# Gate passes inside two attentions: eight at every second step instead of four at each step

## The chip, the cores and the metric

One core of one Trainium2 chip runs the whole program. The metric is the device time of one execution in microseconds (us); lower is better. The core's engines are named as in the profile: PE (matmuls), PEld (its weight loads), DVE (VectorE), ACT (ScalarE), POOL (GpSimd) and SP (which issues most transfers).

## What is computed

Two layers of a decoder trunk over 512 tokens of width 1024. In each layer four mixers (A a gated delta rule, B a latent attention, C a second delta rule, D a sparse attention over selected keys) read the normed input `h`; each mixer's output is projected to 1024 columns and weighted by its own sigmoid gate, which is a projection of `h` too. Cut to what matters here:

```python
p_gdn, p_mla, p_rwkv, p_dsa, p_gate = _split(h @ w_in[l], SLAB_SPLITS)
y_b = mla_mixer(p_mla, ...) @ w_out_mla[l]      # causal attention, 4 heads, 512 keys
y_d = dsa_mixer(p_dsa, ...) @ w_out_dsa[l]      # attention over 128 selected keys per query
g_a, g_b, g_c, g_d = _split(jax.nn.sigmoid(p_gate), GATE_SPLITS)
merged = g_a * y_a + g_b * y_b + g_c * y_c + g_d * y_d
x = x + merged @ w_o[l]
```

## The kernel before

Everything lies transposed in SBUF: 128 features on the partitions, 512 tokens along the row. The weights are cut into units of 1024 x 128, which the kernel takes in one fixed order (`unit_list`). For each unit SP loads a ring slot, ACT rounds it into a high part `w_hi` (L1197), POOL subtracts to get the low part `w_lo` (L462, two instructions), and PE makes 24 passes of 512 columns: 8 slices times high weights on `h_hi`, high weights on `h_lo`, low weights on `h_hi`. There are two slots for `w_hi` and `w_lo`, so ACT may round unit n+2 when PE is through with unit n.

All engines follow orders written out by hand and meet at semaphores. There are two attentions in each layer, "m" (mixer B) and "d" (mixer D), four in the program. Each has 16 tasks, one for each block of 128 queries and head: tasks 0 to 3 are 128 keys wide, 4 to 7 are 256, 8 to 11 are 384, 12 to 15 are 512. The loop has steps i = 0 to 18. The letters below stand for its parts.

- **S(i), S(i+1)**: at even i below 16 PE computes the scores of tasks i and i+1 (L790, L791). In "m" these contract over 96 rows and run one after the other; in "d" over 64 rows and side by side.
- DVE, at its own step i: **ss(i)** adds the mask and takes the row maximum (L1733), and then **n(i-1)** divides the task before by its row sum (a reciprocal, L1741, and a product from SBUF to SBUF, L1742). So n(j) of an odd task j stands behind ss(j+1) on DVE, and ss(j+1) waits for the scores that PE computes at step j+1.
- ACT, at its step i: **exp(i)** with its row sum (L1238); then the copy of the transposed task i-2 (L1245).
- **T(j)**: at step i = j+2 PE transposes task j into a bank of PSUM (L801, one matmul per 128 keys); it waits for n(j).
- **G**: gate passes, at each of the steps 1 to 18 a piece of four. `gate_pieces` (L596) makes three gate units in 18 pieces; L605 and L606 are high-weight passes, L611 are low-weight ones. They write the one bank `bank_f`. After the sixth piece of a unit ACT copies the bank (L1179) and rounds the next weight unit (L1197); the next unit's first pass waits for that copy.
- **Y(i-4)**: at even i from 4 on PE multiplies tasks i-4 and i-3 with the values (L812, tile 128x64) behind the gate piece; ACT copies the result (L1251).

The order on PE in a pair of steps, i even, is therefore: S(i), S(i+1); T(i-2); G; Y(i-4); T(i-1); G; and again. In "m" DVE also works on the selection of keys for mixer D at steps 5, 7, 9, 11 and 13 (`SPARE`; its lines are L2006 to L2021). At step 1 DVE merges one tile ("m") or two ("d") of the branch before.

Of the kernel before, what the change touches and what calls it, by code (L numbers as in the profile page):

```python
# [80 lines left out]
NU = len(UNITS)  # L81


GATE_STEPS = tuple(range(1, 19))


SPARE = {5: 1, 7: 2, 9: 1, 11: 2, 13: 2}
# [82 lines left out]
def build(nc, x_in, pos_in, wstream, par_in, const_in, tabs, x_dram, out):  # L170
    ctx = ExitStack()
    with ctx:
# [34 lines left out]
        def ar(q, shape, at=0):  # L207

            n = int(np.prod(shape))
            v = arena[:, q * T + at:q * T + at + n]  # L210
            if len(shape) == 1:
                return v
            names = " ".join("abcd"[:len(shape)])
            return v.rearrange(f"p ({names}) -> p {names}", **{k: s for k, s in zip("abcd", shape)})
# [81 lines left out]
        class Banks:  # L296
# [8 lines left out]
            def next(self, pool, done, value=None):  # L305


                i = self.used[pool] % len(self.pools[pool])
                self.used[pool] += 1
                sem_, emptied = self.reader[pool][i]  # L310
                if value is None:
                    self.counts[key[done]] = self.counts.get(key[done], 0) + 1
                    value = self.counts[key[done]]
                self.reader[pool][i] = (S[done], value)
                return self.pools[pool][i], sem_, emptied
# [23 lines left out]
        def quarter(i):  # L339

            return slice(i * C, (i + 1) * C)

        def merges_to(g):
# [29 lines left out]
        Dv = dict(  # L373
            rl=ar(11, (4, T)), scores=ar(2, (3, T)), wk=ar(5, (T,)), gt=ar(6, (T,)), eq=ar(30, (T,)), cum=ar(31, (T,)), bias=ar(7, (TT, T)),
            iq=ar(15, (4, T)), q=ar(19, (2, T)), k=ar(21, (2, T)), vf=ar(23, (2, T)), v=ar(25, (TT, 256)), tab=ar(27, (2, T)), ik=ar(29, (T,)),
            tmp=ar(35, (T,)), ss=ar(11, (4, T)), pt=ar(15, (4, TT, P)),
        )
        Mv = dict(
            cq=ar(37, (2, T)), sq=ar(39, (3, T)), rs=ar(23, (2, T)), q=ar(39, (4, T)), k=ar(11, (4, T)), v=ar(43, (TT, 256)),
            tab=ar(27, (2, T)), tmp=ar(29, (T,)), bias=ar(32, (T,)), kr=ar(33, (T,)), qr=ar(34, (T,)),  # L380
            ss=ar(15, (4, T)), pt=ar(33, (4, TT, P)),
        )
# [95 lines left out]
        def _(pe):  # L478
# [88 lines left out]
            def merge_outputs(slot, numbers):  # L567
                for n in numbers:
                    b, reader, emptied = banks.next("v", "mg_done")
                    pe.wait_ge(reader, emptied)  # L570
                    pe.wait_ge(out_here[n % OUT_RING], 16 * (n // OUT_RING + 1))
                    for k in range(2):
                        ins = mm(b[:], out_ring[:, n % OUT_RING, k, :], yo[:, slot, k, :], start=k == 0, stop=k == 1)  # L573
                    ins.then_inc(v_full, 1)

            def unit_pieces(l, wants, done):

                for want in wants:
                    g = begin_unit(want, l)
                    b, reader, emptied = banks.next("f", done)  # L580
                    pe.wait_ge(reader, emptied)
                    hi, lo = w_hi[:, g % SPLIT], w_lo[:, g % SPLIT]
                    for k in range(KT):
                        mm(b[:], hi[:, k, :], h_hi[:, k, :], start=k == 0, stop=False)  # L584
                        mm(b[:], hi[:, k, :], h_lo[:, k, :], start=False, stop=False)
                        if k in (0, 2, 3, 5, 6):
                            yield
                    pe.wait_ge(S["split_lo"], g + 1)
                    for k in range(KT):
                        ins = mm(b[:], lo[:, k, :], h_hi[:, k, :], start=False, stop=k == KT - 1)  # L590
                        if k in (1, 3):
                            yield
                    ins.then_inc(f_full, 1)
                    yield

            def gate_pieces(l, br, i, numbers):  # L596

                for j in range(3):
                    g = begin_unit(("merge", br, i + j), l)
                    numbers.append(merges_to(g))  # L600
                    b, reader, emptied = banks.next("f", "mg_raw")
                    banks.counts["mg_sig"] += 1
                    pe.wait_ge(reader, emptied)
                    for k in range(KT):
                        mm(b[:], w_hi[:, g % SPLIT, k, :], h_hi[:, k, :], start=k == 0, stop=False)  # L605
                        mm(b[:], w_hi[:, g % SPLIT, k, :], h_lo[:, k, :], start=False, stop=False)  # L606
                        if k % 2 == 1:
                            yield
                    pe.wait_ge(S["split_lo"], g + 1)
                    for k in range(KT):  # L610
                        ins = mm(b[:], w_lo[:, g % SPLIT, k, :], h_hi[:, k, :], start=False, stop=k == KT - 1)  # L611
                        if k == 3:
                            yield
                    ins.then_inc(f_full, 1)
                    yield
# [209 lines left out]
            for l in range(L):  # L825
# [86 lines left out]
                pieces = unit_pieces(l, [("gd", 6), ("gd", 7)], "g_z")  # L912
# [37 lines left out]
                pieces = unit_pieces(l, [("ds", 0), ("ds", 1)], "d_in")  # L950
# [75 lines left out]
                for half in range(2):  # L1026
                    b, reader, emptied = banks.next("a", "m_v")
                    pe.wait_ge(reader, emptied)
                    for t2 in range(2):
# [17 lines left out]
                numbers = []  # L1047
                pieces = gate_pieces(l, 1, 0, numbers)
                attention(l, "m", lambda h, qt: Mv["q"][0:96, h, qt * P:(qt + 1) * P],
                          lambda h, n: Mv["k"][0:96, h, 0:n], lambda i: next(pieces) if i in GATE_STEPS else None,  # L1050
                          lambda: merge_outputs(1, last[1:]))
                numbers.append(gate(l, 1, 3))
                pe.wait_ge(S["m_y"], at(l, "m_y", 8))
# [5 lines left out]
                numbers = []  # L1059
                pieces = gate_pieces(l, 3, 0, numbers)  # L1060
                attention(l, "d", lambda h, qt: Dv["q"][quarter(h % 2), h // 2, qt * P:(qt + 1) * P],
                          lambda h, n: Dv["k"][quarter(h % 2), h // 2, 0:n], lambda i: next(pieces) if i in GATE_STEPS else None,
                          lambda: merge_outputs(0, last))
                numbers.append(gate(l, 3, 3))
                pe.wait_ge(S["d_y"], at(l, "d_y", 8))
# [32 lines left out]
        def _(act):  # L1098
# [56 lines left out]
            sigs = [0]  # L1155
# [11 lines left out]

            def gate_done(i):

                return i in GATE_STEPS and GATE_STEPS.index(i) % 6 == 5  # L1170

            def piecewise_sig(l, i):

                if gate_done(i):
                    act.wait_ge(f_full, filled_f.next())
                    n = sigs[0] + GATE_STEPS.index(i) // 6
                    if n >= GATES:
                        act.wait_ge(S["mg_done"], n - GATES + 1)
                    act_fn(sg[:, n % GATES, :], filled_f.bank()[:], ACT.Copy).then_inc(S["mg_raw"], 1)  # L1179
# [51 lines left out]
            def attention(l, x, V, slot, fill):  # L1231
                steps = [(qt, h) for qt in range(TT) for h in range(H)]
                for i in range(len(steps) + 3):
                    if i < len(steps):
                        qt, h = steps[i]
                        n = (qt + 1) * P
                        act.wait_ge(S[x + "_ss"], at(l, x + "_ss", i + 1))
                        act_fn(V["ss"][:, i % 4, 0:n], V["ss"][:, i % 4, 0:n], ACT.Exp, scale=-1.0, bias=att[:, 0, i % 4:i % 4 + 1],  # L1238
                               accum_out=att[:, 1, i % 4:i % 4 + 1]).then_inc(S[x + "_p"], 1)
                    if 2 <= i < len(steps) + 2:  # L1240
                        j = i - 2
                        qt, h = steps[j]
                        act.wait_ge(a_full, filled.next())
                        b = filled.bank()
                        act_fn(V["pt"][:, j % 4, 0:qt + 1, :], b[:, 0:(qt + 1) * P].rearrange("p (k n) -> p k n", n=P), ACT.Copy).then_inc(S[x + "_pt"], 1)  # L1245
                    fill(i)
                    if i >= 4 and i % 2 == 0:
                        qt, h = steps[i - 4]
                        act.wait_ge(a_full, filled.next())
                        b = filled.bank()  # L1250
                        act_fn(yo[:, slot, h // 2, qt * P:(qt + 1) * P], b[:, 0:P], ACT.Copy).then_inc(S[x + "_y"], 1)  # L1251
                    if gate_done(i):
                        split_next()
# [32 lines left out]
            for l in range(L):  # L1286
# [183 lines left out]
                merge_sig(l)  # L1470
                merge_sig(l)
                attention(l, "d", Dv, 1, lambda i: piecewise_sig(l, i))
                late_sig(l, 6)
                merge_sig(l, 1)
# [16 lines left out]
                for q in range(QUARTERS + 1):  # L1491
                    if q < QUARTERS:
                        for i in range(8):
                            n = 8 * q + i
# [760 lines left out]
```

## Time and profile before

| | |
|---|---|
| median of 3 runs | 2022.46 us (2020.97 to 2022.69) |
| profiled execution: its time | 2020.27 us |
| profiled execution: span, first to last instruction | 2018.4 us |
| granted PE clock, mean | 0.997 |
| PE busy | 1972.0 us, 98% |
| DVE, ACT, POOL busy | 1070.0, 769.5, 734.7 us |
| length of one attention, from S(0) to the next unit | about 40.2 us, four times |

The time of the profiled execution is its span and 1.9 us around it. A timeline row gives start and length in us from the span's start, engine, line, operation, operands, and in brackets how long the engine was idle before it and what ended that. PE overlaps its matmuls, so the distance between the starts of two rows says what the first one cost.

### The profile page before, as it was taken

The page shows a single profiled execution, that of the slowest core. Times are in us where ns is not written, and L with a number is a line of the kernel's source. Part 1 is how long each engine was busy: PE and PEld are TensorE (multiplying, and loading weights), DVE is VectorE, ACT ScalarE, POOL GpSimd, SP SyncE. Part 2 cuts the span into 40 slices and gives each one's busy share as a digit, 9 for nine tenths or more (in the row PEclk, how much of TensorE's full clock was granted, in tenths as well). Part 3 has the DMA queues.
Part 4 walks back from the last instruction along what each step waited for, and adds up shares of the span by engine and source line. Part 5 has one row for each costly group of instructions (what it writes and reads, how often), then busy time and mean ns, then how long its engine had stood idle before and what let it go on. Part 6 is the DMA issues. An engine that isn't in the chain of part 4 may idle for free.

```text
span 2018.4 us, 31679 instructions
## 1 busy us (share of the span) xinstructions
PE 1972.0 (98%) x13092; PEld 1523.0 (75%) x13092; DVE 1070.0 (53%) x1795; ACT 769.5 (38%) x1208; POOL 734.7 (36%) x553
## 2 busy tenths in 40 slices
PE   7999999999999999999999999999999999999997
PEld 5788787766667888888877867776666688888886
DVE  8785555888733422222477656379795342222223
ACT  6443513345343332322354353233444334332323
POOL 3431313422224444444444132243222344444443
PEclk9999999999999999999999999999999999999999
DMA  6220112221322333223332111123122223332322
GB/s 235 84 75 28 58 34 79 80 70 50 123 63 81 114 99 99 94 95 100 95 128 87 42 41 55 44 79 102 53 101 69 68 85 96 101 94 94 103 95 74
DMA packets 52063, 170.01 MB, mean 84 GB/s; under 512 B 5824, under 2 KB 14144, under 8 KB 51280
## 3 DMA queue, kind: packets, MB, share of 16 engines
q1 hardware_dynamic: 50928, 163.97, 25.0%
q0 software_dynamic: 992, 4.02, 0.6%
q8 instruction: 105, 1.72, 0.3%
q14 instruction: 38, 0.31, 0.0%
HBM read 160.88 MB, written 7.08 MB: 83 GB/s over the span
## 4 chain that ended last, share of the span: by engine, by line
PE 89%; DVE 7%; ACT 3%; issue 1%; DMA 0%; POOL 0%; ACTq 0%; SPq 0%; DVEq 0%
PE bank_a L497 14%; PE bank_a L498 13%; PE bank_a L503 13%; PE bank_v L503 7%; PE bank_v L497 7%; PE bank_v L498 7%; PE bank_v L573 5%; PE bank_v L651 3%; PE bank_f L584 1%; PE bank_a L801 1%; DVE mg L1546 1%; PE bank_f L611 1%; PE bank_a L961 1%; PE bank_a L812 1%; PE bank_f L605 1%
## 5 line engine op out<-in xcount | busy, mean ns | idle before, releaser
L462 POOL TENSOR_TENSOR w_lo<-ring,w_hi 128x512 fp32r<-128x512 f32 x536 | 727.0, 1377 | 1186.3 <-ACT w_hi L1197 1177.5
L497 PE MATMUL bank_a<-h_hi,w_hi 128*128 128x512 f32 x1296 | 523.2, 404 | 0.0
L498 PE MATMUL bank_a<-h_lo,w_hi 128*128 128x512 f32 x1296 | 505.3, 390 | 0.0
L1197 ACT ACTIVATE w_hi<-ring 128x1024 fp32r<-128x1024 f32 x268 | 281.5, 1050 | 222.6 <-DVE arena L2141 212.4
L503 PE MATMUL bank_a<-h_hi,w_lo 128*128 128x512 f32 x1296 | 320.4, 389 | 0.0
L497 PEld LDWEIGHTS bank_a<-h_hi,w_hi 128*128 128x128 f32 x1296 | 243.3, 188 | 69.9 <-issue 19.3
L498 PEld LDWEIGHTS bank_a<-h_lo,w_hi 128*128 128x128 f32 x1296 | 243.4, 188 | 57.2 <-issue 8.1
L503 PEld LDWEIGHTS bank_a<-h_hi,w_lo 128*128 128x128 f32 x1296 | 243.2, 188 | 50.5
L497 PE MATMUL bank_v<-parts,w_hi 128*128 128x512 f32 x640 | 251.3, 393 | 1.4 <-DVE parts L2110 1.4
L498 PE MATMUL bank_v<-parts,w_hi 128*128 128x512 f32 x640 | 249.1, 389 | 0.0
L1540 DVE TENSOR_TENSOR sg<-bank_v,sg 128x512 f32<-128x512 f32 x112 | 77.4, 691 | 316.5 <-PE bank_v L503 239.3
L2129 DVE TENSOR_TENSOR arena<-arena 128x512 f32<-128x512 f32 x64 | 44.3, 692 | 245.0 <-ACT arena L1499 245.0
L503 PE MATMUL bank_v<-parts,w_lo 128*128 128x512 f32 x640 | 158.2, 389 | 0.0
L497 PEld LDWEIGHTS bank_v<-parts,w_hi 128*128 128x128 f32 x640 | 120.2, 188 | 29.0 <-DVE parts L2110 4.1
L503 PEld LDWEIGHTS bank_v<-parts,w_lo 128*128 128x128 f32 x640 | 120.2, 188 | 25.0
L498 PEld LDWEIGHTS bank_v<-parts,w_hi 128*128 128x128 f32 x640 | 120.2, 188 | 24.9 <-issue 0.5
L1499 ACT ACTIVATE arena<-bank_a 128x512 f32<-128x512 f32 x64 | 38.3, 598 | 205.6 <-PE bank_a L503 205.6
L573 PE MATMUL bank_v<-yo,out_ring 128*128 128x512 f32 x256 | 115.2, 595 | 0.0
L1164 ACT ACTIVATE sg<-bank_a 128x512 f32<-128x512 f32 x52 | 31.1, 597 | 198.2 <-PE bank_a L503 198.1
L1540 DVE TENSOR_TENSOR arena<-arena 128x512 f32<-128x512 f32 (+3 forms) x71 | 92.1, 1297 | 9.6 <-ACT arena L1262 7.3
L573 PEld LDWEIGHTS bank_v<-yo,out_ring 128*128 128x128 f32 x256 | 47.7, 189 | 53.7 <-issue 52.0
L651 PE MATMUL bank_v<-arena 64*64 64x64 f32 x2176 | 66.0, 219 | 2.9 <-ACT arena L1117 2.5
(295 smaller groups left out, 2483.2 us busy)
## 6 DMA issues: line engine op xcount, KB each, us to landing
ring<-in_w SPq DMA_DIRECT2D x268, 512.0 KB, 3.5
out_ring<-in_w SPq DMA_DIRECT2D x64, 128.0 KB, 3.4
x_dram<-arena SPq DMA_DIRECT2D x2, 2048.0 KB, 9.7
arena<-x_dram SPq DMA_DIRECT2D x2, 2048.0 KB, 9.6
arena<-in_x SPq DMA_DIRECT2D x2, 1024.0 KB, 9.3
out_x<-arena SPq DMA_DIRECT2D x4, 512.0 KB, 4.0
consts<-in_const SPq DMA_DIRECT2D x1, 1253.0 KB, 13.8
arena<-tabs POOLq DMA_DIRECT2D x2, 512.0 KB, 4.2
```

The costliest lines, as they stand in the source:

```text
L462: ins = nc.gpsimd.tensor_tensor(w_lo[:, g % SPLIT, ks, :], raw, w_hi[:, g % SPLIT, ks, :].bitcast(F32), ALU.subtract)
L497: mm(b[:], w_hi[:, s, k, :], hi[:, k, :], start=k == 0, stop=False)
L498: mm(b[:], w_hi[:, s, k, :], lo[:, k, :], start=False, stop=False)
L503: ins = mm(b[:], w_lo[:, s, k, :], hi[:, k, :], start=False, stop=k == KT - 1)
L573: ins = mm(b[:], out_ring[:, n % OUT_RING, k, :], yo[:, slot, k, :], start=k == 0, stop=k == 1)
L584: mm(b[:], hi[:, k, :], h_hi[:, k, :], start=k == 0, stop=False)
L651: ins = mm(b[quarter(p_), k * C:(k + 1) * C], lhs[quarter(p_), m, :], rhs(m, p_), start=True, stop=True)
L1164: act_fn(sg[:, n % GATES, :], b[:], ACT.Sigmoid).then_inc(S["mg_sig"], 1)
L1197: act_fn(w_hi[:, g % SPLIT, :, :], ring[:, g % RING, :, :], ACT.Copy).then_inc(S["split_hi"], 1)
L1499: act_fn(relu[:, n % 2, :], b[:], ACT.Relu).then_inc(S["up_relu"], 1)
L1540: link(v.tensor_tensor(out_, a, b, op))
L2129: v.tensor_tensor(relu2[:, n % 2, :], relu[:, n % 2, :], relu[:, n % 2, :], MUL).then_inc(S["up_sq"], 1)
```

## The change

The set of steps with gate passes is halved and each takes two pieces. The pieces keep their order, sizes and number. ACT's copy of the finished gate and its rounding of the next weights move with them, from steps 6, 12, 18 to steps 5, 11, 17.

```diff
-GATE_STEPS = tuple(range(1, 19))
+GATE_STEPS = tuple(range(1, 18, 2))
...
-                          lambda h, n: Mv["k"][0:96, h, 0:n], lambda i: next(pieces) if i in GATE_STEPS else None,
+                          lambda h, n: Mv["k"][0:96, h, 0:n], lambda i: [next(pieces) for _ in range(2)] if i in GATE_STEPS else None,
...
-                return i in GATE_STEPS and GATE_STEPS.index(i) % 6 == 5
+                return i in GATE_STEPS and GATE_STEPS.index(i) % 3 == 2
...
-                    n = sigs[0] + GATE_STEPS.index(i) // 6
+                    n = sigs[0] + GATE_STEPS.index(i) // 3
```

The call for "d" is changed in the same way. On PE a pair of steps becomes: S(i), S(i+1); T(i-2); Y(i-4); T(i-1); G, G.

## Rows read from the trace of the kernel before

**Rows 1.** Page, part 1: busy time, share of the span, instructions.

```profile
PE 1972.0 (98%) x13092; PEld 1523.0 (75%) x13092; DVE 1070.0 (53%) x1795; ACT 769.5 (38%) x1208; POOL 734.7 (36%) x553
```

**Rows 2.** Busy time in the first "m" and "d": us, PE, PEld, DVE, ACT, POOL, PEclk.

```profile
457.38:497.54 40.16, 38.62 (x229) 26.84 (x227) 34.32 (x99) 21.76 (x62) 8.45 (x6) 1.00 0.16 53
535.38:575.56 40.18, 38.84 (x233) 24.11 (x233) 18.85 (x68) 23.24 (x63) 7.53 (x6) 1.00 0.19 63
```

**Rows 3.** Waits of PE in the whole span: us in total, times, longest.

```profile
PE bank_a L801 <- DVE arena L1742: 5.6, 6, 1.3
```

**Rows 4.** Timeline of PE in "d": T(1), then S(4) to T(3).

```profile
543.34 0.30 PE L801 MATMUL bank_a<-consts,arena 128*128 128x128 f32 x1 [1.29 <-DVE arena L1742]
...
544.50 0.48 PE L790 MATMUL bank_v<-arena 64*128 64x256 f32 x1
...
545.21 0.48 PE L605 MATMUL bank_f<-h_hi,w_hi 128*128 128x512 f32 x1
545.53 0.39 PE L606 MATMUL bank_f<-h_lo,w_hi 128*128 128x512 f32 x1
545.76 0.40 PE L605 MATMUL bank_f<-h_hi,w_hi 128*128 128x512 f32 x1
...
546.32 0.44 PE L812 MATMUL bank_a<-arena 128*64 128x128 f32 x4
546.69 0.33 PE L801 MATMUL bank_a<-consts,arena 128*128 128x128 f32 x1
```

**Rows 5.** Timeline of PE in "d": steps 7, 12 and 13.

```profile
550.17 0.44 PE L801 MATMUL bank_a<-consts,arena 128*128 128x128 f32 x2
550.65 0.47 PE L605 MATMUL bank_f<-h_hi,w_hi 128*128 128x512 f32 x1
...
560.02 0.69 PE L790 MATMUL bank_v<-arena 64*128 64x512 f32 x1
...
562.49 0.88 PE L812 MATMUL bank_a<-arena 128*64 128x128 f32 x12
563.30 0.55 PE L801 MATMUL bank_a<-consts,arena 128*128 128x128 f32 x3
563.74 0.47 PE L605 MATMUL bank_f<-h_hi,w_hi 128*128 128x512 f32 x1
```

**Rows 6.** Timeline of DVE in "d": n(3); ss(12), n(11).

```profile
545.77 0.29 DVE L1742 TENSOR_SCALAR arena<-arena,att 128x128 f32<-128x128 f32 x1
...
561.18 0.69 DVE L1733 CUSTOM_DVE_ANT_0 arena<-bank_v,arena 128x512 f32<-128x512 f32 x1 [2.34 <-PE bank_v L791]
...
561.99 0.42 DVE L1742 TENSOR_SCALAR arena<-arena,att 128x384 f32<-128x384 f32 x1
```

**Rows 7.** Timeline of ACT in "m" at step 6: gate copy, Y copy, rounding.

```profile
469.63 0.60 ACT L1179 ACTIVATE sg<-bank_f 128x512 f32<-128x512 f32 x1 [0.15 <-PE bank_f L611]
470.13 0.27 ACT L1251 ACTIVATE yo<-bank_a 128x128 f32<-128x128 f32 x1
470.28 1.06 ACT L1197 ACTIVATE w_hi<-ring 128x1024 fp32r<-128x1024 f32 x1
```

**Rows 8.** Timeline of POOL behind that rounding.

```profile
471.42 2.52 POOL L462 TENSOR_TENSOR w_lo<-ring,w_hi 128x512 fp32r<-128x512 f32 x2 [10.98 <-ACT w_hi L1197]
```

**Rows 9.** Timeline of DVE in "m": selection, ss(8), n(7); later ss(14).

```profile
469.76 0.56 DVE L2006 MAX8 m<-arena 128x8 f32<-128x384 f32 x1
...
472.31 0.56 DVE L1733 CUSTOM_DVE_ANT_0 arena<-bank_v,arena 128x384 f32<-128x384 f32 x1
...
472.99 1.10 DVE L1742 TENSOR_SCALAR arena<-arena,att 128x256 f32<-128x256 f32 x1
...
488.76 0.69 DVE L1733 CUSTOM_DVE_ANT_0 arena<-bank_v,arena 128x512 f32<-128x512 f32 x1
```

**Rows 10.** Timeline of PE in "m": T(7), and T(13).

```profile
474.49 0.44 PE L801 MATMUL bank_a<-consts,arena 128*128 128x128 f32 x2
...
490.20 0.63 PE L801 MATMUL bank_a<-consts,arena 128*128 128x128 f32 x4 [0.73 <-DVE arena L1742]
```

More of the change, by code:

```diff
@@ L1061, in _ @@
                 attention(l, "d", lambda h, qt: Dv["q"][quarter(h % 2), h // 2, qt * P:(qt + 1) * P],
-                          lambda h, n: Dv["k"][quarter(h % 2), h // 2, 0:n], lambda i: next(pieces) if i in GATE_STEPS else None,
+                          lambda h, n: Dv["k"][quarter(h % 2), h // 2, 0:n], lambda i: [next(pieces) for _ in range(2)] if i in GATE_STEPS else None,
                           lambda: merge_outputs(0, last))
```

## The prediction

> **What bounds the kernel now.** I read the page first: PE is busy for 1972.0 of 2018.4 us [rows 1], so time is lost or won only where PE's sequence gets longer, shorter or waits. Then the busy time by stretch: the first "m" and the first "d" take 40.16 and 40.18 us, with PE busy for 38.62 and 38.84 of them and the clock at 1.00, its full level of 2.4 GHz [rows 2]; layer two repeats both within 0.05 us, so each term below counts twice. In "m" DVE is busy for 34.32 us, in "d" for 18.85. Third, the waits: T waits for n in 6 places, for 5.6 us [rows 3]. Last, the timelines of the two attentions, to learn how close each odd T comes to its n.
>
> The reader is to see a chain in them. At an even step i PE computes S(i); DVE can start ss(i) only then, and n(i-1) stands behind ss(i); T(i-1) needs n(i-1). Between S(i) and T(i-1) PE has T(i-2), four gate passes and Y(i-4) to do, and these cover the chain. In "d" at step 4: S at 544.50, T(3) at 546.69 [rows 4]; n(3) ends at 545.77 + 0.29 = 546.06 [rows 6]. T(1) shows how soon T follows its n: it started at 543.34, 0.15 us behind the end of n(1). So T(3) could have started at 546.21, and the slack was 0.48 us. At step 12, n(11) ends at 562.41 [rows 6], T(11) could have started at 562.56 and started at 563.30 [rows 5]: slack 0.74. The six odd tasks 3 to 13 of "d" have slacks from 0.48 to 0.77, growing with the width, leaving aside that POOL lengthened two of the n (below).
>
> **Part 1: passes leave the cover.** A pass costs 0.23 us (545.53 to 545.76, rows 4), four cost 0.92. The change takes four out of the stretch from S(i) to T(i-1) and puts them behind T(i-1). If nothing waited, this would be neutral. But the stretch can shrink by its slack only; the four passes behind T(i-1) are paid in full. Each odd T from 3 to 13 therefore loses 0.92 minus its slack, where the slack is less.
> The Trainium skill (TensorE: Matmul & The Clock Gate, Back-to-back issue gap) gives about 216 ns for a warm gap of 512 columns; the row has 230 and decides. By 216 the four passes would be 0.86, and the sum below some 1 us smaller.
>
> "d": 0.44 + 0.40 + 0.27 + 0.29 + 0.18 + 0.15 = 1.73 us for tasks 3, 5, 7, 9, 11, 13. Task 1 loses nothing: T(1) already waits 1.29 us [rows 4] for n(1), which stands behind the two merges on DVE, and these do not move; the earlier gate passes run inside that wait. Task 15 loses nothing: no S comes ahead of it, n(15) waits for no scores, and the passes of steps 17 and 18 already follow each other today.
>
> "m": the scores run one after the other, so the cover is longer. Slacks by the same reading are 0.75 and about 0.75 for tasks 3 and 5 (loss 0.17 and 0.15), 1.05 and 1.35 for tasks 9 and 11 (no loss but 0.02 each). Tasks 7 and 13 are DVE's, below.
>
> **Part 2: changes of operand kind.** In a pair today PE goes T, G, Y, T, G; after, T, Y, T, G. The first pass behind T takes 0.32 until the second instead of 0.23 [rows 4], and Y starts 0.10 late behind a gate pass (545.76 to 546.32 for two): some 0.16 per pair saved in "d", 0.10 in "m". The change to Y (tile 128x64) directly behind T is in no row; the nearest is Y to T. Four Y products take 0.37 until T (546.32 to 546.69), twelve 0.81 (562.49 to 563.30, rows 5), so each adds 0.055 and the change itself 0.15. Bounds 0 and 0.15; I take 0.12, nearly all of the saving. In 28 pairs (7 in each attention) that is 28 x 0.0 to 28 x 0.13 = 3.6 us of gain. But it lies in the stretch that shrinks, and where T then waits for n, a faster stretch gives nothing: of my pairs only "m" task 9 is not waiting. Cost: 0.
>
> **Part 3: the bank of the gates.** The first pass of a unit waits for ACT's copy of `bank_f`. T(5) is at 550.17 and the pass at 550.65, 0.48 later where 0.20 is usual; at 563.30 and 563.74 it is 0.44 against 0.30 [rows 5]. After the change S, T, Y and T lie between the last pass of a unit and the first of the next, over 2 us, against 0.60 for the copy [rows 7]. This wait goes: 0.42 us in "d", 0.28 in "m" (the second copy is in time there).
>
> **Part 4: ACT and POOL move.** The copy (0.50 to the next) and the rounding (1.05, rows 7) now come at steps 5 and 11, directly behind the eighth pass, where before exp and copies of step 6 or 12 preceded them. Queued behind them on ACT: exp(6), the copies of T(4) and of Y(2), exp(7), the copy of T(5). Y(4), the first on PE to need the last of these, comes some 5 us behind the eighth pass and they need about 4.2; hidden, with 0.8 to spare. At step 17 the rounding passes the copy of Y(14); PE's gate unit of 24 passes hides that.
> POOL starts when the rounding ends plus 0.08 [rows 7, 8]. That is 1.83 us behind S(i) of the next even step in "m", 1.72 in "d". The n of that step starts behind S(12) at 1.16 (561.18 - 560.02) + 0.81 (561.99 - 561.18) = 1.97 [rows 5, 6], so POOL is first by 0.14 and 0.25 us. What this does, the rows show: n(7) in "m" took 1.10 instead of 0.35 us, beginning inside POOL's pair of instructions (471.42 to 473.94) and ending at 474.09 [rows 8, 9]. So n(11) ends when POOL's first instruction of 1.27 is done: T(11) can start 3.4 us behind S(12) in "d" (1.72 + 1.27 + about 0.25 + 0.15) instead of 2.54: +0.86. In "m" it is 3.5 against an arrival of 2.98: +0.52. At step 6 the n(5) is narrower and starts 1.0 us behind S(6), ahead of POOL.
> The Trainium skill (SBUF — State Buffer, Who interferes with whom) calls this an exclusive lock on a pair of ports, held by whoever starts first for the whole instruction; the 1.10 us agrees, and by that rule the order of 0.14 and 0.25 decides the term.
>
> **Part 5: DVE in "m".** n(6) now stands behind exp(6), late by the rounding, and meets POOL: it ends 3.3 us behind S(6). Two rounds of selection follow it (469.76 to 472.31, 2.5 us; rows 9), then ss(8), 0.67 to n(7), 0.35 and 0.14: T(7) at S(6) + 6.93. S(8) comes at S(6) + 3.78, so S(8) to T(7) is 3.15 against 3.12 today (474.49, rows 10). Loss 0.92 + 0.03 - 0.28 (the bank) = 0.67. T(13) waits 0.73 today since ss(14) starts at 488.76 only, behind the selection of step 13, which POOL lengthens [rows 9, 10]. After, POOL works earlier, that selection is undisturbed but starts later: I get ss(14) at 490.0, T(13) at 491.45, which is 0.28 less loss than the tasks before had piled up.
>
> **Sum.** "d": 1.73 - 0.42 + 0.86 = 2.17. "m": 0.17 + 0.15 + 0.67 + 0.02 + 0.54 - 0.28 = 1.27. Two layers: 2 x 3.44 = 6.9 us. Behind each attention PE has no wait that could take this back: DVE idles 5.0 us ahead of the second attention and works its merges off during full gate units. The profiled execution would go from 2020.27 to 2027.2, a span of 2025.3; it lay 2.2 us below the median, so the median would go from 2022.46 to 2029.3. A difference below 0.2%, 4.0 us, I call no change.
>
> **Rivals.** (a) No collision: n(11) gets in ahead of POOL. "d" then loses 1.31. In "m" T(13) hangs on DVE anyway, its 1.25 stays. Together 5.1 us; with the slacks 0.1 larger than read (20 places, 2 us) about 3. For it: margins of only 0.14 and 0.25; against: waits repeated to 0.02 us between the layers. (b) Nothing to tell: T follows n 0.1 sooner than read and the chain is 0.1 shorter, in 20 places each, and no collision in "d": 6.9 - 2 - 2 - 1.7 = 1.2 us. (c) The other side: the order of PE decides, not the chain. If n is in time at every odd T, the change gives only its savings: 3.6 for the kinds and 2 x (0.42 + 0.28) = 1.4 for the bank, 5.0 us faster. It decides from the point where S to n takes no longer than T, Y and their changes, 1.2 us at step 4 of "d"; the rows have 1.71 (546.21 - 544.50). (d) DVE falls behind in "m" (34.32 of 40.16 busy), each selection ends later than S comes, and no slack is usable: the bound is 24 odd tasks x 0.92 = 22 us, I take half, 11.
>
> **Chances.** Forecast 0.45; (a) 0.25, of which 0.15 above 4 us; (b) 0.14; (c) 0.08; (d) 0.08. Slower 0.45 + 0.15 + 0.08 = 0.68; within 0.2% 0.10 + 0.14 = 0.24; faster 0.08. Range: (c) and half of (b) are left out below, the upper end of (d) above: +0.8 to +10 us, 2023.3 to 2032.5. The unknown T-to-Y change moves it little, the collision by 2 x 1.4.
>
> **What the profile after would show.** T waits for L1742 in some 20 places instead of 6, each 0.1 to 0.5 us, one of about 1 us per "d" at T(11) with an n(11) of over 1 us. S(4) to T(3) in "d" 1.71 instead of 2.19. The first pass of the second unit no longer late behind T. Each attention 1 to 2 us longer, "d" more than "m"; the rest of the span alike. Wrong would be: PE reaching the odd T behind n (then c), or DVE's selection pushing ss by more than 1 us (d).

## The result, and the profile after

The changed kernel takes 2027.12 us (median of 11 runs, 2025.89 to 2027.64), the kernel before 2020.97 us (11 runs beside them, 2019.47 to 2022.69): ratio 1.0029, 95% interval 1.002 to 1.0037. It is slower by 6.15 us. That is more than the 0.2% (4.0 us) that counted as a difference, and the lower end of the interval lies just at it. The forecast was +6.9 us. It named 2029.3 us since it started from a median of 2022.46 of three runs; the eleven have 1.5 us less. In the profiled executions the span goes from 2018.4 to 2025.4 us (forecast 2025.3). That closeness is in part luck: 1.1 of these 7.0 us lie outside the attentions, as shown below.

The page's busy times, to be held against [rows 1], and the first of PE's waits [rows 3]:

```profile
PE 1971.9 (97%) x13092; PEld 1526.4 (75%) x13092; DVE 1069.1 (53%) x1795; ACT 767.5 (38%) x1208; POOL 734.4 (36%) x553
```

```profile
PE bank_a L801 <- DVE arena L1742: 11.8, 22, 1.3
```

PE does the same 13092 matmuls in the same busy time; what is new is time in which it stands still. T waits for n in 22 places instead of 6, for 11.8 us instead of 5.6. The 6.2 us more are nearly the whole result. (They are not quite the same thing. The idle time in a bracket counts from the modelled end of the row before it, so it understates a delay: T(3) of "d" came 0.44 us late with 0.38 in its bracket. And the waits for the bank that went away had no bracket of their own. The losses by step, further below, are the better measure.) The windows of the four attentions ("m", "d", and the same in layer two; columns as in [rows 2]):

```profile
457.56:498.64 41.08, 38.51 (x229) 27.61 (x227) 33.29 (x99) 21.74 (x63) 8.17 (x6) 1.00 0.15 52
536.49:578.69 42.20, 38.71 (x233) 25.02 (x232) 19.47 (x68) 23.16 (x64) 7.71 (x6) 1.00 0.19 59
1453.06:1494.15 41.09, 38.50 (x230) 27.60 (x228) 33.32 (x99) 21.74 (x63) 8.19 (x6) 1.00 0.16 51
1531.99:1574.17 42.18, 38.69 (x234) 25.02 (x233) 19.46 (x68) 23.16 (x64) 7.70 (x6) 1.00 0.19 59
```

An "m" has grown from 40.16 to 41.08 us, a "d" from 40.18 to 42.20 [rows 2], the clock is at its full level in both. The four together went from 160.66 to 166.55, by 5.89 us. The spans differ by 7.0, but what lies outside the attentions takes between 1857.5 and 1860.1 us in the eleven traces of this study, and which kernel lies where in this range doesn't follow the edits; so the sum of the attentions is the better reading of one profile, and each experiment below is judged by it first. It agrees with the medians.

Step 4 of "d" on PE, then on DVE, the counterpart of [rows 4] and [rows 6]:

```profile
546.51 0.48 PE L790 MATMUL bank_v<-arena 64*128 64x256 f32 x1
...
547.14 0.33 PE L801 MATMUL bank_a<-consts,arena 128*128 128x128 f32 x1
547.41 0.44 PE L812 MATMUL bank_a<-arena 128*64 128x128 f32 x4
548.22 0.30 PE L801 MATMUL bank_a<-consts,arena 128*128 128x128 f32 x1 [0.38 <-DVE arena L1742]
548.28 2.09 PE L611 MATMUL bank_f<-h_hi,w_lo 128*128 128x512 f32 x8
```

```profile
547.25 0.42 DVE L1733 CUSTOM_DVE_ANT_0 arena<-bank_v,arena 128x256 f32<-128x256 f32 x1 [2.31 <-PE bank_v L791]
547.60 0.08 DVE L1733 DVE_READ_ACCUMULATOR2_ANT att<- 128x1 f32 x1
547.60 0.16 DVE L1741 RECIPROCAL att<-att 128x1 f32<-128x1 f32 x1
547.79 0.29 DVE L1742 TENSOR_SCALAR arena<-arena,att 128x128 f32<-128x128 f32 x1
```

No gate pass stands between S(4) and T(3) any more, and T(3) waits 0.38 us for n(3). S(4) to T(3) is 1.71 us, the length of the chain as read beforehand, against 2.19 before. All eight passes follow behind T(3), so four more than before are paid there (0.92 us) and only 0.48 is won in front of it.

Step 12 of "d", ACT, POOL, DVE and PE:

```profile
563.21 0.60 ACT L1179 ACTIVATE sg<-bank_f 128x512 f32<-128x512 f32 x1 [0.83 <-PE bank_f L611]
563.70 1.05 ACT L1197 ACTIVATE w_hi<-ring 128x1024 fp32r<-128x1024 f32 x1
```

```profile
564.83 2.63 POOL L462 TENSOR_TENSOR w_lo<-ring,w_hi 128x512 fp32r<-128x512 f32 x2 [10.21 <-ACT w_hi L1197]
```

```profile
565.07 1.25 DVE L1742 TENSOR_SCALAR arena<-arena,att 128x384 f32<-128x384 f32 x1
```

```profile
563.10 0.69 PE L790 MATMUL bank_v<-arena 64*128 64x512 f32 x1
...
566.47 0.52 PE L801 MATMUL bank_a<-consts,arena 128*128 128x128 f32 x3 [0.95 <-DVE arena L1742]
566.74 0.47 PE L605 MATMUL bank_f<-h_hi,w_hi 128*128 128x512 f32 x1
```

ACT rounds directly behind the eighth pass, POOL begins 0.24 us ahead of n(11), and n(11) takes 1.25 us in place of 0.42 [rows 6]. T(11) starts 3.37 us behind S(12) (forecast 3.4). The gate pass behind it comes 0.27 after it, in place of 0.44 [rows 5]: the wait for the bank is gone.

In "m" the selection holds up T(7). DVE and PE there, the counterpart of [rows 9] and [rows 10]:

```profile
471.11 0.80 DVE L1742 TENSOR_SCALAR arena<-arena,att 128x256 f32<-128x256 f32 x1
471.84 0.55 DVE L2006 MAX8 m<-arena 128x8 f32<-128x384 f32 x1
...
474.32 0.56 DVE L1733 CUSTOM_DVE_ANT_0 arena<-bank_v,arena 128x384 f32<-128x384 f32 x1
...
489.87 0.69 DVE L1733 CUSTOM_DVE_ANT_0 arena<-bank_v,arena 128x512 f32<-128x512 f32 x1
```

```profile
472.52 0.81 PE L790 MATMUL bank_v<-arena 96*128 96x384 f32 x2
...
475.50 0.41 PE L801 MATMUL bank_a<-consts,arena 128*128 128x128 f32 x2 [0.72 <-DVE arena L1742]
...
491.32 0.52 PE L801 MATMUL bank_a<-consts,arena 128*128 128x128 f32 x3 [0.39 <-DVE arena L1742]
```

PE starts S(8) at 472.52, but ss(8) starts at 474.32 only, when two rounds of selection are done.

How much later each odd T starts than before, counted from S(0) of its attention (so T(3) of "d": 548.22 - 536.49 = 11.73 against 546.69 - 535.38 = 11.31), gives the loss of each step, beside the forecast, us:

| | T(1) | T(3) | T(5) | T(7) | T(9) | T(11) | T(13) | end | sum |
|---|---|---|---|---|---|---|---|---|---|
| "d" measured | -0.02 | 0.44 | 0.38 | -0.02 | 0.29 | 0.99 | -0.02 | -0.02 | 2.02 |
| "d" forecast | 0 | 0.44 | 0.40 | -0.01 | 0.29 | 1.04 | 0.01 | 0 | 2.17 |
| "m" measured | 0 | 0.18 | 0.17 | 0.48 | -0.04 | 0.51 | -0.36 | -0.02 | 0.92 |
| "m" forecast | 0 | 0.17 | 0.15 | 0.67 | 0.02 | 0.54 | -0.28 | 0 | 1.27 |

(A minus sign is a step that lost nothing and gave some of the earlier loss back. The forecast's bank terms stand where they fall: in "d" 0.28 at T(7) and 0.14 at T(13), in "m" in T(7).)

### The profile page after: what moved, and what is told of

Read it like the earlier page. It is cut to its first block, busy times and chain, and to the rows that moved or that the text cites. A ratio compares the mean times of both kernels' runs of the same rounds, so it can differ in the third digit from the quotient of the medians.

```text
span 2025.4 us, 31679 instructions
## 1 busy us (share of the span) xinstructions
PE 1971.9 (97%) x13092; PEld 1526.4 (75%) x13092; DVE 1069.1 (53%) x1795; ACT 767.5 (38%) x1208; POOL 734.4 (36%) x553
## 4 chain that ended last, share of the span: by engine, by line
PE 87%; DVE 7%; ACT 3%; issue 2%; DMA 0%; POOL 0%; ACTq 0%; SPq 0%; DVEq 0%
PE bank_a L497 13%; PE bank_a L498 13%; PE bank_a L503 13%; PE bank_v L503 7%; PE bank_v L497 7%; PE bank_v L498 7%; PE bank_v L573 5%; PE bank_v L651 3%; PE bank_f L611 1%; PE bank_f L584 1%; DVE mg L1546 1%; PE bank_a L961 1%; PE bank_f L590 1%; PE bank_a L801 1%; PE bank_f L605 1%
## 5 line engine op out<-in xcount | busy, mean ns | idle before, releaser
L1540 DVE TENSOR_TENSOR sg<-bank_v,sg 128x512 f32<-128x512 f32 x112 | 77.4, 691 | 315.8 <-PE bank_v L503 239.4
L1540 DVE TENSOR_TENSOR arena<-arena 128x512 f32<-128x512 f32 (+3 forms) x71 | 90.2, 1271 | 9.6 <-ACT arena L1262 7.3
```

Source lines behind the costliest of these rows:

```text
L1540: link(v.tensor_tensor(out_, a, b, op))
```

## The experiments

Nine kernels were tried. None leaves anything out; they change the order of work alone. The theory: PE's order is worth little itself. What costs time is the part of the chain from S by ss and n to T that exceeds the work in front of T, plus the two collisions (POOL with n(11), the selection with T(7)). The main rivals: more per pass moved than the chain explains (blocks of eight cost by themselves), or gains from fewer changes of kind. The columns: the attentions "m" and "d" in layer one; the sum of all four and its difference to before; and the difference of the medians against the runs of before on the same chip:

| kernel | "m" | "d" | all four | four, to before | median, to before |
|---|---|---|---|---|---|
| before | 40.16 | 40.18 | 160.66 | | |
| the change | 41.08 | 42.20 | 166.55 | +5.89 | +6.15 |
| eight at even steps | 39.09 | 39.74 | 157.73 | -2.93 | -2.61 |
| rounding later | 40.96 | 41.38 | 164.67 | +4.01 | +4.33 |
| change, n ahead of ss | 39.79 | 39.52 | 158.64 | -2.02 | -1.95 |
| before, n ahead of ss | 40.00 | 40.00 | 159.99 | -0.67 | -0.34 |
| both of them | 40.12 | 39.93 | 160.13 | -0.53 | -0.62 |
| six and two | 40.82 | 41.05 | 163.76 | +3.10 | +2.59 |
| less selection at 7 | 39.89 | 42.21 | 164.22 | +3.56 | +3.58 |
| two moved, rounding later | 39.87 | 39.52 | 158.79 | -1.87 | -1.50 |
| even steps, n(1) first | 39.11 | 39.90 | 158.03 | -2.63 | -2.52 |

**Blocks of eight at the even steps.** The same blocks, put where they stand between S(i) and T(i-1). On PE: S, S, T(i-2), eight G, Y, T(i-1).

```diff
-GATE_STEPS = tuple(range(1, 18, 2))
+GATE_STEPS = tuple(range(2, 19, 2))
```

> Eight passes at each even step 2 to 18 instead of at each odd step: the blocks of eight stay, but they stand between S(i) and T(i-1) again. Chain theory (the passes left the cover of ss(i) and n(i-1)): the waits of odd T for n go back to about those of before, T(14) in "m" waits some 0.7 us for n(14) in their place, the bank wait stays away; 1 to 3 us faster than the kernel before, 7 to 9 below the changed kernel. Rival (blocks of eight, or fewer and larger pieces, cost by themselves; or ACT's and POOL's work collides wherever the block ends): stays about 6 us above the kernel before.

2018.08 us (2017.08 to 2019.48), ratio to before 0.9989 (0.998 to 0.9997), so some 9 us below the changed kernel. From T(3) on no T waits. That answers the rival that the block costs by itself: what costs is the side of T on which it stands. A wait at T(14) of "m" was expected, from POOL meeting the selection; it did not come. POOL and DVE there:

```profile
484.79 1.50 POOL L462 TENSOR_TENSOR w_lo<-ring,w_hi 128x512 fp32r<-128x512 f32 x1 [11.22 <-ACT w_hi L1197]
484.79 2.93 POOL L462 TENSOR_TENSOR w_lo<-ring,w_hi 128x512 fp32r<-128x512 f32 x2 [11.22 <-ACT w_hi L1197]
```

```profile
484.19 0.56 DVE L1540 TENSOR_TENSOR arena<-arena 128x384 f32<-128x384 f32 x1
484.78 0.36 DVE L2021 TENSOR_SCALAR arena<-arena 128x384 f32<-128x384 f32 x1
```

DVE's last long instruction of the selection was done at 484.75, and the short one behind it began 0.01 us ahead of POOL and took its usual 0.36. Here it is POOL that grew: its first instruction took 1.50 us in place of 1.27, and the pair 2.93 in place of 2.52. (The first row is the first instruction alone, the second the pair; the rest of the growth came later, when n(13) stood beside the pair.) It is the race of n(11) with the other winner.

**The rounding one step later.** In the changed kernel ACT keeps the copy of the gate bank where it is, and rounds behind the next step's work.

```diff
-                    if gate_done(i):
+                    if gate_done(i - 1):
```

> The changed kernel with ACT's rounding of the next weights one step later (end of steps 6, 12, 18); the copy of the gate bank stays at 5, 11, 17. Collision theory (POOL's low part holds up n(11)): T(11) waits 0.2 instead of 0.95 us in each "d" and 0 instead of 0.44 in each "m"; "d" 0.75 shorter each, "m" 0 to 0.4, since POOL then meets the selection of step 13; 1.5 to 2.4 us below the changed kernel. Rival (the wait at T(11) is the chain alone, n(11) is long for another reason): no difference to the changed kernel, +6 us.

2025.02 us (2023.41 to 2026.29), ratio 1.002 (1.0012 to 1.0029). In "d" T(11) does not wait and the attention is 0.82 shorter: the term of 0.86, by itself. The waits at T(3), T(5), T(7) and T(9) stay as they were (0.38, 0.33, 0.25, 0.21). In "m" the waits at T(7) and T(11) are gone, but "m" is only 0.12 shorter: T(13) now waits 1.51, for POOL meets the selection of step 13. POOL and DVE in that kernel:

```profile
485.25 3.15 POOL L462 TENSOR_TENSOR w_lo<-ring,w_hi 128x512 fp32r<-128x512 f32 x2 [11.33 <-ACT w_hi L1197]
```

```profile
485.83 1.45 DVE L1546 SCALAR_TENSOR_TENSOR arena<-arena,sml 128x384 f32<-128x384 f32 x1
487.31 1.50 DVE L1540 TENSOR_TENSOR arena<-arena 128x384 f32<-128x384 f32 x1
```

These take 0.62 and 0.56 us when POOL is idle (488.23 and 488.88 in the changed kernel's trace). A collision that is moved is still a collision.

**n(i-1) ahead of ss(i) at even steps**, in the changed kernel and in the kernel before. The chain of an odd T loses ss, and n no longer needs the scores:

```diff
+                    if i >= 2 and i % 2 == 0:
+                        normalise(i - 1)      # L1741, L1742 for task i-1
...                                            # wait for the scores, ss(i)
-                    if i >= 1:
+                    if i % 2 == 1:
```

> The changed kernel, but DVE does n(i-1) ahead of ss(i) at each even step, so that n of an odd task no longer stands behind scores that PE has yet to make. Chain theory: the waits of odd T for n go, but for T(7) and T(13) in "m" (selection), T(1) comes 0.4 us sooner; 0 to 3 us faster than the kernel before, 6 to 9 below the changed kernel. Rival (the order on PE itself costs: T directly followed by Y, blocks of eight): stays within 1 us of the changed kernel, +5 to +6.

> The kernel before with the same exchange on DVE. Chain theory: before, the cover was long enough, so the exchange can give only T(1), 0.4 us in each of four attentions, and T(13) in "m", some 0.6 in each of two: 1.5 to 3 us faster than the kernel before. If it gives as much here as on the changed kernel (6 or more), the exchange is a gain of another kind and says nothing on the cover.

The changed kernel with the swap takes 2018.74 us (2017.97 to 2020.29), ratio 0.9991 (0.9982 to 1.0); the kernel before with it 2020.35 (2019.88 to 2021.15), ratio 0.9999 (0.999 to 1.0008). With n out of reach of S, the order of PE that cost 6 us costs none: every wait from T(3) on is gone but one of 0.44 in "m", T(7). Step 4 of "d" on PE, in the changed kernel with the swap:

```profile
544.86 0.48 PE L790 MATMUL bank_v<-arena 64*128 64x256 f32 x1
...
545.49 0.33 PE L801 MATMUL bank_a<-consts,arena 128*128 128x128 f32 x1
545.75 0.44 PE L812 MATMUL bank_a<-arena 128*64 128x128 f32 x4
546.12 0.33 PE L801 MATMUL bank_a<-consts,arena 128*128 128x128 f32 x1
```

S(4) to T(3) without any wait is 1.26 us; rival (c) had 1.2 for it. It also settles what the changes of kind are worth. Its "d" is 0.66 shorter than before, of which 0.22 is T(1), which comes sooner (7.74 us behind S(0) in place of 7.96), and 0.42 the bank as read beforehand; 0.02 is left for all seven pairs. The steps say the same: where no bank term falls (T(3), T(5), T(9), T(11)), the distance from one odd T to the next is within 0.03 us of before, and where one falls (T(7), T(13)) it is 0.33 and 0.13 shorter. In the kernel before, the swap gave 0.67 us where 1.5 to 3 were expected: T(1) comes 0.2 sooner each time, T(13) of "m" 0.96, and then T(14) waits 0.62, since ss and exp of the even task now stand behind n.

**Both of them**, blocks at even steps and the swap:

> Blocks of eight at even steps and n(i-1) ahead of ss(i) on DVE, the two variants that beat the kernel before, put together. Chain theory: both remove the same wait, so they don't add up; only T(1) comes 0.2 us sooner in each attention: 2 to 4 us faster than the kernel before, 0 to 1 below the even-step variant alone. Rival (the two gains are of different kinds and add): 5 us or more below the kernel before.

2020.25 us (2019.13 to 2021.99), ratio 0.9998 (0.9989 to 1.0007). Expected were 2 to 4 us below the kernel before, and 0 to 1 below the blocks at even steps alone; it is 0.6 below the one and some 2 above the other. The two gains do not add, they undo each other: T(14) in "m" waits 0.83 and T(2) in "d" 0.3. At an even step of this order T(i-2) has no gate pass ahead of it, and the swap has made its ss and exp later by an n. In "m" that n(13) meets POOL too and takes 1.20 us (at 488.34) in place of 0.49.

**Pieces of six and two**, with the gate steps of the kernel before: two passes of each four are moved out of the cover.

```diff
 # passes in a piece, from step 1: 4, 4, ...  ->  6, 2, 6, 2, ...
-                        if k % 2 == 1:
+                        if k in (2, 3, 6, 7):
-                        if k == 3:
+                        if k == 5:
```

> The kernel before with pieces of six passes at odd steps and two at even ones, so that two passes (0.46 us) leave the cover and not four. Chain theory: loss of a task is the passes moved minus its slack, and slacks in "d" are 0.48 and more, in "m" more: no loss, attentions within 0.1 us of the kernel before, total 0 to +0.5 us. Rival (each pass moved costs its share): half of the changed kernel's loss, some +3 us.

2023.46 us (2022.21 to 2025.76), ratio 1.0012 (1.0003 to 1.0021), where next to nothing was expected. By its total alone the rival would be right, that each pass moved costs its share: it had said some +3 us. The trace tells them apart. The odd T wait in the same 6 places as before, for 6.5 us in place of 5.6, and only T(13) of "m" waits longer. Most of the loss sits where I had not looked, at the bank. PE's waits for it in the whole span (the kernel before has none in this list), and then PE and ACT in "d":

```profile
PE bank_f L605 <- ACT sg L1179: 2.1, 6, 0.4
```

```profile
550.36 0.44 PE L801 MATMUL bank_a<-consts,arena 128*128 128x128 f32 x2
551.22 0.47 PE L605 MATMUL bank_f<-h_hi,w_hi 128*128 128x512 f32 x1 [0.42 <-ACT sg L1179]
```

```profile
549.72 0.51 ACT L1238 ACTIVATE arena<-arena,att 128x256 f32<-128x256 f32 x1 [1.80 <-DVE att L1733]
...
550.23 0.36 ACT L1245 ACTIVATE arena<-bank_a 128x256 f32<-128x256 f32 x1
550.49 0.59 ACT L1179 ACTIVATE sg<-bank_f 128x512 f32<-128x512 f32 x1
```

The last piece of a unit has only two passes, and the bank's copy stands behind exp(6) and the copy of T(4) on ACT. The first pass of the next unit comes 0.86 us behind T(5), in place of 0.48 in the kernel before and 0.20 where the bank is free; for the second unit it is 0.91 behind T(11) in place of 0.44. Together they are nearly all of the 0.87 that "d" lost. In "m" the bank costs 0.22 and T(13) the other 0.44: it waits 1.17 in place of 0.73, for the selection of step 13 meets POOL over more of its length (its L1546 and L1540 take 1.58 and 1.51 us).

**Less selection at step 7.** The changed kernel, with the two rounds of selection of step 7 put behind the others, outside the attention.

```diff
-SPARE = {5: 1, 7: 2, 9: 1, 11: 2, 13: 2}
+SPARE = {5: 1, 9: 1, 11: 2, 13: 2}
...
-                go_on(9)
+                go_on(11)
```

> The changed kernel with the two rounds of selection taken from step 7 of "m" and done behind the attention. If T(7) in "m" is late because selection stands between the delayed n(6) and ss(8): T(7) waits under 0.1 instead of 0.72 us, "m" is 0.7 shorter, twice; 1.4 us below the changed kernel unless the selection is then missed ahead of "d". Rival (T(7) is late through exp(6) alone, behind the rounding): T(7) still waits 0.7 us and nothing changes.

2024.45 us (2023.49 to 2026.16), ratio 1.0018 (1.0009 to 1.0027). "d" is as in the changed kernel (42.21), "m" 1.19 shorter: T(7) comes 0.8 us sooner and does not wait, and neither does T(13). Step 7's selection is what holds up T(7), but not alone: with the rounding one step later it stands in the same place and T(7) does not wait either. It takes both, the early rounding, which makes n(6) late, and the selection behind n(6). This is a measure of the cause rather than an offer: DVE is busy in the window for 30.81 us in place of 33.29.

**Two passes moved, the rounding later**: six and two again, but with the units ending on the pieces of six, and the rounding as in the second experiment. Only two passes leave the cover, and the bank has time. The gate steps are 1 to 17 here, each with one piece; the diff is against the kernel before, cut to the sizes of the pieces:

```diff
 # passes in a piece, from step 1: 8, then 2 at even and 6 at odd steps
-                        if k % 2 == 1:
+                        if k in (3, 4, 7) or (k == 0 and j):
-                        if k == 3:
+                        if k == 1:
```

> The changed kernel with its rounding one step later, and only two of the eight passes taken out of the cover: pieces of six at the odd steps and of two at the even ones. The chain theory (ss, n and T of an odd step wait only for what exceeds the passes in front of them): in attention d the spare time in front of the odd T's was 0.48 us or more, and two passes are 0.46 us, so the odd T's wait 0.05 us at most and the attention takes 39.7 to 39.9 us, against 41.38 in the kernel with the later rounding; in m the wait at T(13) by the selection and GpSimd stays, about 1 us. Span 2020 to 2021.5. The rival, that each pass that leaves the cover costs its share: d about 40.6, span 2022.5.

2018.71 us (2017.78 to 2020.7), ratio 0.9992 (0.9983 to 1.0001). "d" takes 39.52 us, below the 39.7 to 39.9 expected and far from the rival's 40.6; no odd T but T(1) waits in it, which itself waits 0.82 in place of 1.29. The span, 2018.9 us, is below the 2020 to 2021.5 expected too. In "m" T(13) waits 1.18. Of the 1.86 us against "rounding later" (41.38), 0.47 is T(1), in whose wait two more passes now run, which I had not counted; the other 1.39 are the odd tasks behind it, whose waits were 1.17 by their brackets. Two of four passes brought back into the cover take all of that loss away: it is not a share for each pass but an excess over the slack. That also answers the rival whose total came out with six and two.

**Blocks at even steps, n(1) alone ahead of ss(2).** In that order T(1) of "d" has the longest wait left, 1.30 us; here it is mended by itself.

> Blocks of eight at even steps, and VectorE's n(1) alone ahead of ss(2). The chain theory: T(1), which waits 0.6 us in m and 1.3 us in d, comes 0.2 us sooner in each of the four attentions, nothing is given back later, since T(2) has eight gate passes ahead of it: 0.8 us below the kernel with blocks of eight at even steps at best, 3 to 4 us below the kernel before. The rival, as with the swap at every even step: the exp of step 2 comes later by n(1) and T(2) then waits as much: no gain over blocks at even steps alone.

2017.69 us (2016.45 to 2018.17), ratio 0.9987 (0.9978 to 0.9995), not to be told from the blocks alone (0.9989). T(1) of "d" does come 0.21 sooner, and T(2) gives it back; in "m" T(1) comes no sooner, for in that order it stands behind eight passes and does not wait. PE in "d":

```profile
541.16 0.30 PE L801 MATMUL bank_a<-consts,arena 128*128 128x128 f32 x1 [1.09 <-DVE arena L1727]
...
542.41 0.30 PE L801 MATMUL bank_a<-consts,arena 128*128 128x128 f32 x1 [0.32 <-DVE arena L1727]
542.47 0.47 PE L605 MATMUL bank_f<-h_hi,w_hi 128*128 128x512 f32 x1
```

(L1727 is here what L1742 is elsewhere.) The expectation had eight gate passes ahead of T(2). They stand behind it: at an even step T comes first. The rival was right, and the sum of the four is even 0.30 longer than without the swap.

## Why the prediction was right

- **What bounds it.** PE's order and waits; nothing else moved. Right: the waits of T for n grew by 6.2 us, the time by 6.15, the four attentions by 5.89.
- **Part 1, the cover.** Right in kind and size. The chain reads 1.71 us at step 4 of "d" before and after; the plain tasks 3, 5 and 9 of "d" lost 0.44, 0.38 and 0.29 us for 0.44, 0.40 and 0.29. The swap shows that it is the chain: out of it, no loss. Two passes moved show that it is an excess: no loss either.
- **Part 2, changes of kind at 0.** Right, and for one more reason than was given. They are worth 0.02 in a "d" even where nothing waits. (The rows shown give 0.09 + 0.10 = 0.19 per pair of "d" for what is saved, where the prediction has some 0.16; nothing hung on it.) S(4) to T(3) takes 1.26 us there: T, Y and their changes eat what the pair saves elsewhere (T to Y 0.26). Rival (c), 5.0 us faster, counted 3.6 of its gain from here; where n is in time at nearly every odd T, the gain is 2.0, of which 0.8 is T(1).
- **Part 3, the bank.** Right: no first pass is late in "d" (0.20 and 0.27 behind T), and T(7) and T(13) lost what was forecast with these terms in it (-0.02 for -0.01, -0.02 for 0.01). Six and two is the same term with the sign turned: the copy's place on ACT decides it.
- **Part 4, POOL first.** The narrowest call, margins of 0.14 and 0.25 us, measured as 0.15 ("m": 483.96 to 484.11, rows below) and 0.24. T(11) lost 0.99 for 1.04 in "d" and 0.51 for 0.54 in "m"; the later rounding gives 0.82 back in "d". By the Trainium skill (SBUF — State Buffer, Who interferes with whom) issue order decides which of the two is blocked; the trace agrees from both sides: n(11) loses by 0.15 and takes 1.34 us, and with the blocks at even steps DVE is first by 0.01, keeps its 0.36 us, and POOL's first instruction takes 1.50 in place of 1.27. POOL and DVE in "m":

```profile
483.96 2.63 POOL L462 TENSOR_TENSOR w_lo<-ring,w_hi 128x512 fp32r<-128x512 f32 x2 [10.90 <-ACT w_hi L1197]
484.11 1.34 DVE L1742 TENSOR_SCALAR arena<-arena,att 128x384 f32<-128x384 f32 x1
```

- **Part 5, the selection in "m".** Right in kind; this is the mis-sized term. T(7) was forecast at S(6) + 6.93 and S(8) at S(6) + 3.78; they were at 6.85 and 3.87 (475.50 and 472.52 from 468.65). So 0.48 was lost, not 0.67. T(13) gave 0.36 back, not 0.28, and T(9) 0.04 in place of a loss of 0.02. Together "m" lost 0.92 of 1.27, which is 0.7 of the 1.0 us by which four attentions came out below 6.9; "d" has the other 0.3.
- **What was not foreseen** has no part in the result. Taking one wait away mostly raises another: later rounding, the swap in the kernel before, and n(1) alone each gave back at T(13), T(14) or T(2) a good part of what they won.

What stays open is the time outside the attentions, which differs by up to 2.6 us between single traces; no run was made to tell why. Effects of that size can't be read from the span of one profile.

## What to carry to other kernels

Before filler work is moved on the bound engine, write down for every consumer how long its chain on the other engines is and what stands in front of it; the price is the part of the chain that the cover no longer reaches, not a share of what was moved, and filler put on the right side of the consumer costs nothing and can gain (here the same blocks one step apart take 0.11% less and 0.29% more than the kernel before). Follow also what the moved work releases: a copy and a rounding that came one step sooner put GpSimd 0.2 us ahead of a VectorE instruction, which was 0.82 of the 2.02 us lost in "d". And a wait removed from one task is worth only what the next has as slack, so read the task behind it before counting the gain.

## What the runs showed of the hardware

VectorE's product from SBUF to SBUF (128x384, 0.42 us) took 1.25 us when it began 0.24 us into GpSimd's pair, and 1.34 when it began 0.15 into it; its tensor_tensor of 0.56 us took 1.50 us. Its scores instruction, which reads a bank of PSUM and the mask, took its usual 0.68 us (at 566.24 in "d") while GpSimd was at the second of its pair. GpSimd's pair became longer too, from 2.52 us to 2.63 in the change and to 3.15 where two such VectorE instructions met it. Y directly behind T starts 0.26 us after it (545.49 to 545.75). One, two and three matmuls of T last 0.33, 0.44 and 0.55 us [rows 4, 5], so one more of the same kind is 0.11, and by this estimate the change to Y's tile costs some 0.15: the upper bound of the forecast, not the 0.12 taken.
